# A two-layer transformer block on one NeuronCore: three norms between projections, run in two token halves

## The chip, the cores and the metric

The kernel runs on one core of one Trainium2 chip. The metric is the device time of one execution in microseconds (us). Of an execution the hardware profiler gives a span and, for each instruction, its engine, its start and its duration. The engines are TensorE (PE; its weight loads are PEld), VectorE (DVE), ScalarE (ACT), GpSimd (POOL) and SyncE (SP).

## The reference, cut to what matters

512 tokens of width 1024 go through two layers, all in float32. The three places of this change are where a projection with a residual is followed by an RMS norm and by the next stage's projections:

```python
# seam 1 (norm 1), first layer
x = x + jnp.concatenate([a, b], axis=-1) @ w_out[l]   # a: windowed attention, b: pooling mixer
h2 = rms_norm(x, norm2_g[l])
x = x + peer(h2, ...)                                 # begins with q = h2 @ wq
# rms_norm: y = x * rsqrt(mean(x * x, axis=-1) + eps) * g, each token over its 1024 values
```

Seams 2 and 3 (norms 4 and 6) are in the second part: the output projection of the differential attention (seam 2) and of the short convolution (seam 3), each scaled by a gate and added to x, then a norm with gain and shift, then a feed-forward that begins with its gate and up projections. Every token is normed for itself.

## The kernel before, in words

**Layout.** All activations lie with features on the 128 partitions and tokens along the free axis: x is 8 chunks (`DC = 8`) of 128 features by 512 tokens (`T`). The normed tokens are kept as a sum of two tiles, `hn_hi` and `hn_lo` (a rounded high part and the rest), and so is the input of the output projections, `mix_hi` and `mix_lo`.

**Weight units.** All weights come as 486 units of 128x1024 (`U_WIN` to `N_UNITS`), in the order of their use, through a ring of 8 slots (`RING`). SyncE loads unit u into slot u % 8 once `unit_used` says that unit u - 8 is used. ScalarE makes its high part (`split_hi`, L934), GpSimd its low part (L466), which overwrites the raw data, and TensorE waits for `lo_ready` (`unit_in`). ScalarE splits unit u + 5 (`AHEAD = 5`) when unit u has been used, so five units are ready ahead.

**A unit on TensorE.** `project` runs, for each of 8 chunks, three matmuls over 512 tokens (`mm3`, L494 to L496: high x high, high x low, low x high) into one PSUM bank, and then raises `unit_used`. Each unit gives 128 output features of all 512 tokens.

**The work around a seam.** Order is written out by hand for each engine; semaphores tie them together. The out projection is 8 units into 4 banks in turn. Behind each unit VectorE adds the bank to `x[:, n]` (L1425; with a gate L1689 in `add_projection`) and raises `x_done`; ScalarE splits a unit ahead and then squares chunk n - 1 of x (`square`, L948, called from `splits`); VectorE adds the square to `std` (`square_sum`, L1327). After the eighth unit:

- TensorE: `norm(k)` multiplies `std` by a matrix of ones, which sums over partitions (L515).
- ScalarE takes the square root (L960), VectorE its reciprocal (L1334), all for 512 tokens.
- Per chunk: VectorE scales x by gain and reciprocal into `nrm` (L1348), ScalarE writes the high part (L964, or L966 with a shift), VectorE the low part (L1339 or L1342) and raises `hn_ready`.
- TensorE's first unit of the next stage waits for each chunk in turn (`ready=`).

The next stage is the query projection of the expert layer at seam 1 (16 units, each followed by score matmuls, L602, and top-k work on VectorE, L1437 and below), and the feed-forward (`feed_forward`: `gate_up`, `down`) at seams 2 and 3. Norm 3, of 256 context tokens, runs through the same lines with tiles of 256 columns.

The lines of this order on VectorE and on ScalarE at seam 1 are:

```python
for n in range(DC):                                   # VectorE, L1423 to L1429
    dve.wait_ge(unit_used, U_WOUT + n + 1)
    V.tensor_tensor(x[:, n], ps[:, n % 4, :], x[:, n], ALU.add).then_inc(x_done, 1)
    if n > 1:
        square_sum(1, n - 1)
square_sum(1, DC - 1)
norm(1)

for m in range(n):                                    # ScalarE, splits(u0, n, k), L1029 to L1036
    used(u0 + m)
    split_hi(u0 + m + AHEAD)
    if m:
        square(k, m - 1)
square(k, DC - 1)
```

Of the kernel before, what the change touches and what calls it, by code (L numbers as in the profile page):

```python
# [16 lines left out]
F32 = mybir.dt.float32  # L17
# [3 lines left out]
ALU = mybir.AluOpType  # L21
# [88 lines left out]
def build_program(nc, w_units, x_in, ctx_in, params, consts, consts2, trig, pool_w, subkeys, ada_w, out,  # L110
                  rel_dram, gate_dram, act_dram, x_dram):
    KB = 1024
    with ExitStack() as ctx:
# [145 lines left out]
        SQUARES_BANK = (7, 7, 7, 7, 7, 0, 7)  # L259

# [20 lines left out]
        hn_ready = sem("hn_ready")  # L281
        hn_hi_ready = sem("hn_hi_ready")
# [106 lines left out]
        def _(sp):  # L389
# [43 lines left out]
            sp.wait_ge(hn_ready, 2 * DC)  # L433
# [51 lines left out]
        def _(pe):  # L485
# [25 lines left out]
            def norm(k):  # L511

                W = NORMS[k][1]
                pe.wait_ge(sq_added, (DC - 1) * (k + 1))
                mm(ps[:, SQUARES_BANK[k], :W], ones, std[:, :W], start=True, stop=True).then_inc(mean_ready, 1)  # L515

# [73 lines left out]
            for n in range(DC):  # L590
                if n >= 4:
                    pe.wait_ge(x_done, n - 3)
                project(U_WOUT + n, ps[:, n % 4, :], mix_hi, mix_lo)
            norm(1)


# [10 lines left out]
            for n in range(2 * PEER_HEADS):  # L607
                if n >= 4:
                    pe.wait_ge(q_ev, n - 3)
                project(U_WQ + n, ps[:, n % 4, :], hn_hi, hn_lo, ready=(hn_ready, DC) if n == 0 else None)  # L610
                if n:
                    scores(n - 1)
# [130 lines left out]
            def keys_own(n):  # L743
                unit_in(U_DIFF + n)
                for c in range(DC):
                    if n == 0:
                        pe.wait_ge(hn_ready, 2 * DC + c + 1)
# [3 lines left out]
            def keys_context(n):  # L751
                for c in range(DC):
                    if n == 0:
                        pe.wait_ge(hn_ready, 3 * DC + c + 1)
# [105 lines left out]
            def out_projection(u0, ready, ready0, x0):  # L860
                for n in range(DC):
                    if n >= 4:
                        pe.wait_ge(x_done, x0 + n - 3)
                    project(u0 + n, ps[:, n % 4, :], mix_hi, mix_lo, ready=(ready, ready0) if n == 0 else None)

            def feed_forward(L, U, x0):
                f0 = FF_TILES * L

                def gate_up(g, u, i=None, ready=None):
                    for k in range(2):  # L870
                        f = f0 + 2 * g + k
                        for a, s in ((0, ff_s), (1, ff_p)):
                            if f >= 2:
                                pe.wait_ge(s, f - 1 if i is None else i * 8 + (f - 1))
                            project(u + 2 * k + a, ps[:, 2 * a + k, :], hn_hi, hn_lo, per=24, i=i,
                                    ready=ready if k + a == 0 else None)
# [1045 lines left out]
```

## Time and profile before

| | |
|---|---|
| median of 3 runs | 3458.77 us |
| lowest and highest | 3450.98 and 3459.42 us |
| profiled execution, its own time | 3454.71 us |
| its span | 3452.9 us |
| mean granted clock of TensorE | 0.965 |

A row of the timeline gives the start in us from the span's start, the duration in us, the engine, the line, the operation, what is written from what is read, the shapes, and a count where several equal instructions were merged; square brackets hold the idle time before it and who ended it. A granted clock of 1.00 is 2.4 GHz and of 0.50 is 1.2 GHz. Matmuls are pipelined, so a record is longer than the distance to the next start. Durations on GpSimd are rough.

### The profile page before, as it was taken

To read this page: it belongs to the slowest core of one execution; us is meant where nothing else is said; L and a number is where in the kernel's file an instruction comes from. 1 tells how busy PE (TensorE), PEld (TensorE's weight loads), DVE (VectorE), ACT (ScalarE), POOL (GpSimd) and SP (SyncE) were. 2 spreads that over 40 slices of the span, in tenths; PEclk is the share of its full clock that TensorE was granted. 3 is DMA by queue.
4 is the path that set the end of the run, shared out by engine and by line. 5 is a ranking of instruction groups with operands and counts; after the bars stand their busy time and mean duration, and the time that the engine had idled before them with its cause. 6 is when DMAs were issued, how large, how long until landed. Compare 5 with 4: busy or idle time off the path is not lost.

```text
span 3452.9 us, 41466 instructions
## 1 busy us (share of the span) xinstructions
PE 3254.0 (94%) x14966; PEld 2584.8 (75%) x14966; DVE 1905.2 (55%) x2797; ACT 1099.3 (32%) x1524; POOL 1196.8 (35%) x490
## 2 busy tenths in 40 slices
PE   6689999999999989999999899898889998989999
PEld 4568668888888878888888678544568886868887
DVE  5548894666666525555555671778643336553333
ACT  3332233444444422222222332345322213222221
POOL 3123243333333344444444222100134443434442
PEclk9889999999999999999999999888899999999999
DMA  5022775555555565555555311100222222222222
GB/s 147 32 74 90 276 274 183 187 186 183 191 182 198 183 204 195 192 191 194 194 194 194 125 65 56 43 0 1 67 76 93 99 97 80 98 73 98 98 97 74
DMA packets 191913, 456.22 MB, mean 132 GB/s; under 512 B 11544, under 2 KB 79256, under 8 KB 189208
## 3 DMA queue, kind: packets, MB, share of 16 engines
q1 hardware_dynamic: 86688, 310.57, 26.3%
q10 hardware_dynamic: 105080, 143.66, 12.1%
q8 instruction: 97, 1.59, 0.2%
q14 instruction: 48, 0.39, 0.0%
HBM read 381.31 MB, written 72.88 MB: 132 GB/s over the span
## 4 chain that ended last, share of the span: by engine, by line
PE 83%; DVE 12%; ACT 2%; issue 1%; DMA 0%; ACTq 0%; SPq 0%; DVEq 0%
PE ps L494 25%; PE ps L495 25%; PE ps L496 25%; PE ps L658 3%; DVE nrm L1348 1%; PE ps L832 1%; PE ps L626 1%; DVE std L1327 1%; DVE stats L1601 1%; PE ps L814 1%; DVE Ed L1627 1%; DVE rstd L1334 1%; DVE dec L1484 1%; DVE hn_lo L1342 1%; PE ps L823 0%
## 5 line engine op out<-in xcount | busy, mean ns | idle before, releaser
L466 POOL TENSOR_TENSOR unit_lo<-unit_raw,unit_hi 128x1024 fp32r<-128x1024 f32 x486 | 1196.6, 2469 | 2229.6 <-ACT unit_hi L934 2228.5
L494 PE MATMUL ps<-hn_hi,unit_hi 128*128 128x512 f32 x2248 | 910.2, 405 | 52.4 <-DVE hn_lo L1342 31.7
L495 PE MATMUL ps<-hn_lo,unit_hi 128*128 128x512 f32 x2248 | 883.9, 393 | 0.0
L496 PE MATMUL ps<-hn_hi,unit_lo 128*128 128x512 f32 x2248 | 883.6, 393 | 0.0
L934 ACT ACTIVATE unit_hi<-unit_raw 128x1024 fp32r<-128x1024 f32 x486 | 504.6, 1055 | 661.2 <-DMA unit_raw<-w_units 498.1
L494 PEld LDWEIGHTS ps<-hn_hi,unit_hi 128*128 128x128 f32 x2248 | 426.9, 190 | 198.2 <-issue 69.9
L496 PEld LDWEIGHTS ps<-hn_hi,unit_lo 128*128 128x128 f32 x2248 | 426.8, 190 | 90.8
L495 PEld LDWEIGHTS ps<-hn_lo,unit_hi 128*128 128x128 f32 x2248 | 428.1, 190 | 85.4 <-issue 3.8
L494 PE MATMUL ps<-gp_hi,unit_hi 128*128 128x512 f32 x1024 | 399.3, 390 | 8.4 <-DVE gp_lo L1540 8.4
L495 PE MATMUL ps<-gp_lo,unit_hi 128*128 128x512 f32 x1024 | 399.2, 390 | 0.0
L496 PE MATMUL ps<-gp_hi,unit_lo 128*128 128x512 f32 x1024 | 399.1, 390 | 0.0
L1533 DVE TENSOR_TENSOR gp<-abuf,gbuf 128x512 f32<-128x512 f32 x128 | 232.6, 1818 | 238.6 <-PE ps L496 215.3
L1511 DVE TENSOR_SCALAR hotA<-con,eT 128x128 f32<-128x128 f32 x512 | 344.2, 732 | 0.0
L1704 DVE TENSOR_TENSOR pf<-gel,ps 128x512 f32<-128x512 f32 x44 | 30.3, 688 | 408.8 <-PE ps L496 408.8
L1069 ACT ACTIVATE stage<-ps 128x512 f32<-128x512 f32 x128 | 76.4, 597 | 561.3 <-PE ps L496 550.7
L1507 DVE TENSOR_TENSOR hotB<-con,eT 128x512 f32<-128x512 f32 x128 | 88.3, 690 | 265.6 <-PE ps L658 243.9
L494 PEld LDWEIGHTS ps<-gp_hi,unit_hi 128*128 128x128 f32 x1024 | 192.7, 188 | 48.8 <-issue 8.8
L496 PEld LDWEIGHTS ps<-gp_hi,unit_lo 128*128 128x128 f32 x1024 | 192.6, 188 | 40.1
L495 PEld LDWEIGHTS ps<-gp_lo,unit_hi 128*128 128x128 f32 x1024 | 192.7, 188 | 40.0
L1540 DVE TENSOR_TENSOR gp_lo<-gp,gp_hi 128x512 fp32r<-128x512 f32 x128 | 154.7, 1209 | 117.9 <-ACT gp_hi L1144 117.8
L1276 ACT ACTIVATE gel<-ps 128x512 f32<-128x512 f32 x44 | 26.3, 598 | 513.1 <-PE ps L496 513.1
L1718 DVE SCALAR_TENSOR_TENSOR x<-ps,modraw,x 128x512 f32<-128x512 f32 x176 | 126.4, 744 | 46.3 <-PE ps L496 45.1
(236 smaller groups left out, 3816.6 us busy)
## 6 DMA issues: line engine op xcount, KB each, us to landing
unit_raw<-w_units SPq DMA_DIRECT2D x486, 512.0 KB, 3.3
araw<-ada_units SPq DMA_DIRECT2D x96, 512.0 KB, 6.0
act_dram<-stage ACTq DMA_DIRECT2D x32, 1024.0 KB, 6.1
gate_dram<-gst ACTq DMA_DIRECT2D x16, 2048.0 KB, 8.1
gbuf<-gate_dram ACTq DMA_DIRECT2D x32, 1024.0 KB, 6.3
abuf<-act_dram ACTq DMA_DIRECT2D x32, 1024.0 KB, 9.9
x<-x_t SPq DMA_DIRECT2D x8, 256.0 KB, 6.0
x_dram<-x ACTq DMA_DIRECT2D x1, 2048.0 KB, 8.3
```

Source lines behind the costliest of these rows:

```text
L466: nc.gpsimd.tensor_tensor(lo[:, u % RING], raw[:, u % RING], hi[:, u % RING].bitcast(F32), ALU.subtract).then_inc(lo_ready, 1)
L494: mm(dst, wh, ah, start=start, stop=False)
L495: mm(dst, wh, al, start=False, stop=False)
L496: return mm(dst, wl, ah, start=False, stop=stop)
L658: last = mm(out_t, hotB[:, r % 2, j, :], hotA[:, r % 2, j, :], start=True, stop=True)
L934: activation(hi[:, u % RING], raw[:, u % RING], ACT.Copy).then_inc(hi_ready, 1)
L1069: activation(stage[:, g % 2, u % BUNCH], ps[:, u % 2, :], ACT.Gelu).then_inc(gel_done, 1)
L1507: V.tensor_tensor(hotB[:, r % 2], iota.unsqueeze(1).broadcast_to([P, 4, P]), four.unsqueeze(2).broadcast_to([P, 4, P]), ALU.is_equal)
L1511: last = V.tensor_scalar(hotA[:, r % 2, j, :], iota, eT[:, 0, tok], eT[:, 2, tok], ALU.is_equal, ALU.mult)
L1533: V.tensor_tensor(gp[:, v % 4].rearrange("p (b t) -> p b t", t=TB), abuf[:, g % 2, k].rearrange("p (b t) -> p b t", t=TB), gbuf[:, g % 2, ...
L1540: V.tensor_tensor(gp_lo[:, v % 4], gp[:, v % 4], gp_hi[:, v % 4].bitcast(F32), ALU.subtract).then_inc(p_ready, 1)
L1718: V.scalar_tensor_tensor(x[:, m], ps[:, 4 + m % 4, :], mod(L, 5)[:, m:m + 1], x[:, m], ALU.mult, ALU.add).then_inc(x_done, 1)
```

## The change

At the three seams the out projection, the norm and the first four units of the next stage are run for tokens 0 to 255 (half 0) and 256 to 511 (half 1):

- **TensorE** (`seam_projection`): the eight projection units for half 0, then the same eight for half 1, in three banks in turn; the squares of half 0 are multiplied by ones after the first half-1 unit. Then `seam_units`: the first four units of the next stage for half 0, waiting per chunk for half 0 of the normed tokens, with the squares of half 1 after the first of them; then the same four for half 1. `unit_used` is raised only in the half-1 passes.
- **ScalarE** (`seam`): three splits without a wait for a used unit during the first pass; in the second pass, behind unit n, the square of half 1's chunk n - 1, the high part of half 0's chunk n - 1, and from n = 3 on a split. At seam 1 the load of the sub-keys is issued before the projection instead of after it.
- **VectorE** (`seam`): in the second pass, behind unit n, the add of half 1, the sum of squares of half 1's chunk n - 1, the scaling of half 0's chunk n - 1 and the low part of half 0's chunk n - 2.
- The other four norms keep their code; their semaphore counts are renumbered (`WHOLE`). SyncE's first load of modulation weights waits for the half-counted semaphore. At seam 1 the scores of the first three units run in the half-1 pass (`after`).

The diff, cut to its core (`HALVES` are the two token slices, `SEAM` numbers the three seams):

```diff
+            def seam_projection(k, u0, x0, banks, ready=None):
+                for h in range(2):
+                    for n in range(DC):
+                        j = DC * h + n
+                        if j >= DC + 3:
+                            pe.wait_ge(x_done, x0 + n - 2)
+                        elif j >= 3:
+                            pe.wait_ge(half_added, DC * SEAM[k] + j - 2)
+                        unit_in(u0 + n)
+                        for c in range(DC):
+                            if ready is not None and j == 0:
+                                pe.wait_ge(ready, c + 1)
+                            wh, wl = unit_chunk(u0 + n, c)
+                            last = mm3(ps[:, banks[j % 3], 0:T // 2], wh, wl, mix_hi[:, c, HALVES[h]],
+                                       mix_lo[:, c, HALVES[h]], c == 0, c == DC - 1)
+                        last.then_inc(unit_used if h else half_full, 1)
+                        if j == DC:
+                            seam_mean(k, 0)
+            def seam_units(k, u0, banks, after=None):
+                for h in range(2):
+                    for n, bank in enumerate(banks):
+                        unit_in(u0 + n)
+                        for c in range(DC):
+                            if n == 0:
+                                pe.wait_ge(half_ready, DC * (2 * SEAM[k] + h) + c + 1)
...
+                        if h:
+                            last.then_inc(unit_used, 1)
+                            if n and after is not None:
+                                after(n - 1)
+                        elif n == 0:
+                            seam_mean(k, 1)
...
-                project(U_WOUT + n, ps[:, n % 4, :], mix_hi, mix_lo)
-            norm(1)
+            seam_projection(1, U_WOUT, 0, (4, 5, 6))
...
+            seam_units(1, U_WQ, range(4), after=scores)
...
-            out_projection(U_WO, wo_lo, 0, X_WO)
-            norm(4)
+            seam_projection(4, U_WO, X_WO, (4, 5, 6), ready=wo_lo)
...
+            def seam(k, u0):
+                for n in range(DC):
+                    if n < DC - AHEAD:
+                        split_hi(u0 + n + AHEAD)
+                    if n:
+                        seam_square(k, 0, n - 1)
+                seam_square(k, 0, DC - 1)
+                activation(rstd[:, 0:1], eps, ACT.Sqrt)
+                for n in range(DC):
+                    used(u0 + n)
+                    if n == 0:
+                        seam_root(k, 0)
+                    else:
+                        seam_square(k, 1, n - 1)
+                        seam_high(k, 0, n - 1)
+                    if n >= DC - AHEAD:
+                        split_hi(u0 + n + AHEAD)
+                seam_square(k, 1, DC - 1)
+                seam_high(k, 0, DC - 1)
+                seam_root(k, 1)
+                for c in range(DC):
+                    seam_high(k, 1, c)
...
+            def seam(k, u0, banks, gate=None):
...
+                for n in range(DC):
+                    add(0, n)
+                    if n > 1:
+                        sum_up(0, n - 1)
+                sum_up(0, DC - 1)
+                for n in range(DC):
+                    add(1, n)
+                    if n == 0:
+                        inverse(0)
+                        continue
+                    if n > 1:
+                        sum_up(1, n - 1)
+                    scaled(0, n - 1)
+                    if n > 1:
+                        low(0, n - 2)
+                sum_up(1, DC - 1)
+                scaled(0, DC - 1)
+                low(0, DC - 2)
+                low(0, DC - 1)
+                inverse(1)
+                for c in range(DC):
+                    scaled(1, c)
+                    if c:
+                        low(1, c - 1)
+                low(1, DC - 1)
```

## Rows read from the trace of the kernel before

**Rows 1.** The page's first part: busy time of each engine.

```profile
PE 3254.0 (94%) x14966; PEld 2584.8 (75%) x14966; DVE 1905.2 (55%) x2797; ACT 1099.3 (32%) x1524; POOL 1196.8 (35%) x490
```

**Rows 2.** Timeline of TensorE at seam 1: start, duration, line, operation, [idle before].

```profile
179.04 0.50 PE L494 MATMUL ps<-mix_hi,unit_hi 128*128 128x512 f32 x1 [1.41 <-DVE mix_lo L1420]
...
227.78 2.08 PE L515 MATMUL ps<-std,con 128*128 128x512 f32 x2 [4.91 <-DVE std L1327]
236.28 0.77 PE L494 MATMUL ps<-hn_hi,unit_hi 128*128 128x512 f32 x1 [6.43 <-DVE hn_lo L1339]
...
246.11 0.39 PE L494 MATMUL ps<-hn_hi,unit_hi 128*128 128x512 f32 x1
```

**Rows 3.** Timeline of TensorE, two matmuls of 512 columns, 168 apart.

```profile
183.94 0.39 PE L494 MATMUL ps<-mix_hi,unit_hi 128*128 128x512 f32 x1
...
222.02 0.39 PE L494 MATMUL ps<-mix_hi,unit_hi 128*128 128x512 f32 x1
```

**Rows 4.** Stretches at seam 1: length, busy times, granted clock, DMA share, GB/s.

```profile
224.00:226.00 2.00, 0.00 (x0) 0.00 (x0) 1.49 (x1) 1.98 (x3) 1.97 (x1) 0.72 0.90 307
...
240.00:241.00 1.00, 1.00 (x4) 0.56 (x3) 0.96 (x2) 0.36 (x1) 0.00 (x0) 0.50 0.00 0
...
242.00:244.00 2.00, 1.65 (x6) 0.80 (x6) 1.96 (x4) 0.73 (x2) 0.00 (x0) 1.00 0.00 0
```

**Rows 5.** Timeline of TensorE, two matmuls of 256 columns, 47 starts apart.

```profile
2087.69 0.28 PE L494 MATMUL ps<-unit_hi,cn_hi 128*128 128x256 f32 x1
...
2093.33 0.28 PE L496 MATMUL ps<-unit_hi,cn_lo 128*128 128x256 f32 x1
```

**Rows 6.** Timeline behind a unit of seam 1; last row: GpSimd idle.

```profile
195.70 1.06 ACT L934 ACTIVATE unit_hi<-unit_raw 128x1024 fp32r<-128x1024 f32 x1 [3.86 <-PE ps L496]
...
196.66 0.61 ACT L948 ACTIVATE sq<-x 128x512 f32<-128x512 f32 x1
196.84 2.40 POOL L466 TENSOR_TENSOR unit_lo<-unit_raw,unit_hi 128x1024 fp32r<-128x1024 f32 x1 [3.05 <-ACT unit_hi L934]
197.31 2.47 DVE L1327 TENSOR_TENSOR std<-std,sq 128x512 f32<-128x512 f32 x1 [0.92 <-ACT sq L948]
...
1958.91 0.68 DVE L1327 TENSOR_TENSOR std<-std,sq 128x512 f32<-128x512 f32 x1
```

**Rows 7.** Timeline of GpSimd and VectorE in norm 0, two GpSimd operations merged.

```profile
27.38 5.47 POOL L466 TENSOR_TENSOR unit_lo<-unit_raw,unit_hi 128x1024 fp32r<-128x1024 f32 x2 [4.01 <-ACT unit_hi L934]
...
30.68 2.73 DVE L1348 SCALAR_TENSOR_TENSOR nrm<-x,par,rstd 128x512 f32<-128x512 f32 x1
```

**Rows 8.** Timeline of GpSimd and VectorE in the first feed-forward, merged rows.

```profile
2561.95 10.11 POOL L466 TENSOR_TENSOR unit_lo<-unit_raw,unit_hi 128x1024 fp32r<-128x1024 f32 x4 [6.12 <-ACT unit_hi L934]
...
2569.71 3.52 DVE L1718 SCALAR_TENSOR_TENSOR x<-ps,modraw,x 128x512 f32<-128x512 f32 x5
```

**Rows 9.** Timeline of norm 3, whose tiles have 256 columns.

```profile
1987.83 0.47 ACT L960 ACTIVATE std<-ps,con 128x256 f32<-128x256 f32 x1 [1.83 <-PE ps L515]
...
1988.33 1.75 DVE L1334 RECIPROCAL rstd<-std 128x256 f32<-128x256 f32 x1 [1.82 <-ACT std L960]
1990.12 0.88 DVE L1348 SCALAR_TENSOR_TENSOR nrm<-cT,gmod,rstd 128x256 f32<-128x256 f32 x2
...
1990.64 0.91 ACT L966 ACTIVATE cn_hi<-nrm,gmod 128x256 fp32r<-128x256 f32 x2 [2.34 <-DVE nrm L1348]
```

**Rows 10.** Seam 2: the last low parts; second unit of the feed-forward.

```profile
2462.97 1.47 DVE L1670 TENSOR_TENSOR mix_lo<-Od,mix_hi 128x512 fp32r<-128x512 f32 x2
...
2527.39 0.40 PE L494 MATMUL ps<-hn_hi,unit_hi 128*128 128x512 f32 x1
```

**Rows 11.** Seam 3: the last low part beside GpSimd; second unit of the feed-forward.

```profile
3029.72 2.39 POOL L466 TENSOR_TENSOR unit_lo<-unit_raw,unit_hi 128x1024 fp32r<-128x1024 f32 x1 [3.05 <-ACT unit_hi L934]
...
3029.84 2.83 DVE L1759 TENSOR_TENSOR mix_lo<-yc,mix_hi 128x512 fp32r<-128x512 f32 x1
...
3095.95 0.39 PE L494 MATMUL ps<-hn_hi,unit_hi 128*128 128x512 f32 x1
```

**Rows 12.** Timeline of VectorE in the query projection: the top-k behind a unit.

```profile
259.00 0.89 DVE L1437 MAX8 vals<-ps 128x8 f32<-128x128 f32 x4 [1.11 <-PE ps L602]
```

More of the change, by code:

```diff
@@ L513, in norm, with seam_mean @@
                 W = NORMS[k][1]
-                pe.wait_ge(sq_added, (DC - 1) * (k + 1))
+                pe.wait_ge(sq_added, (DC - 1) * (WHOLE[k] + 1))
                 mm(ps[:, SQUARES_BANK[k], :W], ones, std[:, :W], start=True, stop=True).then_inc(mean_ready, 1)
+            def seam_mean(k, h):
+                pe.wait_ge(half_summed, (DC - 1) * (2 * SEAM[k] + h + 1))
+                mm(ps[:, SQUARES_BANK[k], HALVES[h]], ones, std[:, HALVES[h]], start=True, stop=True)\
+                    .then_inc(half_mean, 1)
@@ L606, in _ @@
             pe.wait_ge(subk_in, 16)
[L607 to L612, printed above, removed]
+            seam_units(1, U_WQ, range(4), after=scores)
+            for n in range(4, 2 * PEER_HEADS):
+                pe.wait_ge(q_ev, n - 3)
+                project(U_WQ + n, ps[:, n % 4, :], hn_hi, hn_lo)
+                scores(n - 1)
             scores(2 * PEER_HEADS - 1)
@@ L858, in _, with gate_up @@
             at_squares(HEADS - 1)
[L860 to L864, printed above, removed]
             def feed_forward(L, U, x0):
                 f0 = FF_TILES * L
-                def gate_up(g, u, i=None, ready=None):
+                def gate_up(g, u, i=None):
                     for k in range(2):
@@ L872, in gate_up @@
                         for a, s in ((0, ff_s), (1, ff_p)):
[L873 to L876, printed above, removed]
+                            pe.wait_ge(s, f - 1 if i is None else i * 8 + (f - 1))
+                            project(u + 2 * k + a, ps[:, 2 * a + k, :], hn_hi, hn_lo, per=24, i=i)
                 def down(g, u, i=None):
@@ L1027, in _ @@
                            ACT.Copy).then_inc(swa_hi, 1)
-            def splits(u0, n, k):
-                for m in range(n):
-                    used(u0 + m)
-                    split_hi(u0 + m + AHEAD)
-                    if m:
-                        square(k, m - 1)
-                square(k, DC - 1)
-            splits(U_WOUT, DC, 1)
+            act.wait_ge(swa_lo, TT)
             act.dma_start(subk[:, :, :], subkeys).then_inc(subk_in, 16)
-            norm(1)
+            seam(1, U_WOUT)
             o, w = PAR["c"]
@@ L1291, in feed_forward @@
                     split_hi(U + 64 + k + AHEAD)
-            splits(U_WO, DC, 4)
-            norm(4)
+            seam(4, U_WO)
             feed_forward(0, U_FF0)
@@ L1304, in _ @@
                     split_hi(U_SC + 3 * j + a + AHEAD)
-            splits(U_SCO, DC, 6)
-            norm(6)
+            seam(6, U_SCO)
             feed_forward(1, U_FF1)
@@ L1421, in _ @@
                                 mix_hi[:, 0:4, tok].bitcast(F32), ALU.subtract).then_inc(swa_lo, 1)
-            for n in range(DC):
-                dve.wait_ge(unit_used, U_WOUT + n + 1)
-                V.tensor_tensor(x[:, n], ps[:, n % 4, :], x[:, n], ALU.add).then_inc(x_done, 1)
-                if n > 1:
-                    square_sum(1, n - 1)
-            square_sum(1, DC - 1)
-            norm(1)
+            seam(1, U_WOUT, (4, 5, 6))
             V.memset(cact[:, :, :], 0.0).then_inc(cact_made, 1)
@@ L1736, in _ @@
                 dve.wait_ge(loaded, 16)
-            add_projection(U_WO, mod(0, 2), 4)
-            norm(4)
+            seam(4, U_WO, (4, 5, 6), mod(0, 2))
             feed_forward(0, U_FF0, X_FF0)
@@ L1759, in _ @@
                 V.tensor_tensor(mix_lo[:, j], yc[:, b], mix_hi[:, j].bitcast(F32), ALU.subtract).then_inc(sc_done, 1)
-            add_projection(U_SCO, mod(1, 2), 6)
-            norm(6)
+            seam(6, U_SCO, (6, 4, 5), mod(1, 2))
             feed_forward(1, U_FF1, X_FF1)
```

114 lines of the change are left out of this document (85 added, 29 removed).

## The prediction

> **What bounds the kernel now.** TensorE: the page's first part has it busy for 94% of the span [rows 1]. I looked next at what it does around one of the three norms, in the timeline. At the first seam the eight units of the out projection start at 179.04, the matmul over the squares comes at 227.78 after 4.91 us of idleness, the first matmul on the normed tokens at 236.28 after 6.43 more, and the second unit of the next stage at 246.11 [rows 2]. A unit is 24 matmuls of 512 columns; the gap from 183.94 to 222.02 is 168 of them, so 0.2267 us each and 5.44 a unit [rows 3]. Nine units should take 49.0 us, and 246.11 - 179.04 is 67.1: 18 us are lost at this seam, in idleness and in a first unit fed chunk by chunk. The stretches show the granted clock: it falls to 0.50 (1.2 GHz) in the gap, stays there with TensorE waiting, and is 1.00 (2.4 GHz) again from about 242, some 5.5 us after work resumed [rows 4]. The two other seams look alike. So there is something to win, at most 3 x 18 us; the question is what the halves cost and whether the vector work fits beside them.
>
> **What the halves cost on TensorE.** A matmul of 256 columns starts every (2093.33 - 2087.69) / 47 = 0.120 us [rows 5], so a half unit is 2.88 us and a whole one in halves 5.76, 0.32 more. Twelve units a seam run in halves: 3.8 us a seam, 11.5 in all. The Trainium skill (TensorE: Matmul & The Clock Gate, "Back-to-back issue gap") gives N/2.4 + 2.5 ns, about 109 and 216 ns; by that the halving would cost an estimated 2 us in all. The rows disagree with it, and the rows decide.
>
> **The lock between VectorE and GpSimd.** Every weight unit needs a high part (ScalarE, L934) and then a low part (GpSimd, L466, 2.40 us). In the timeline of the first seam the split starts at 195.70, GpSimd at 196.84, the square ends at 197.27, and the add of squares std+sq, started at 197.31, takes 2.47 us where it takes 0.68 with GpSimd idle: it ends 0.54 us after GpSimd's end at 199.24 [rows 6]. All six such adds beside a low part in each seam look so. The loser waits for the whole instruction. The same holds for a scaling (L1348: 2.73 instead of 0.75), and after two queued GpSimd operations it shows VectorE getting its turn between them [rows 7]. Adds out of PSUM pass untouched: five of L1718 in 3.52 us while GpSimd runs from 2561.95 to 2572.06 [rows 8]. Before, one such wait per 5.44 us unit was hidden.
>
> In the second half pass of the new order this is on the chain. From the fourth unit on ScalarE does, in this order: square(n-1) of half 1, high part of chunk n-1 of half 0, split of weights; VectorE does add, sum, scaling, low part. The split releases GpSimd (2.40), the square after it releases the sum, which meets the lock each time; the scaling stands behind the sum on VectorE, the high part behind the scaling, and the next split behind the high part on ScalarE. One round, from GpSimd's start to its next: 2.40, then 0.27 until the scaling starts (half of the 0.54 above, the width being half), 0.48 + 0.04 for it, 0.41 from the start of the high part to the split behind it (two of 256 columns in 0.91 us), and 1.14 from the split to GpSimd's start (196.84 - 195.70): 4.74 us [rows 6, 9]. TensorE needs only 2.88. There are five splits, so four rounds.
>
> **The chain of a later seam**, counted from T0, the end of the first half pass. Eight half units and the matmul over squares (about 0.5, a quarter of the 2.08 us of [rows 2]: half the columns, twice the clock): second pass ends at 23.5. The fourth of its units ends at 12.0; add, sum, scaling and high part (0.48 + 0.42 + 0.48 + 0.40, with 0.2 of handing over) bring the first split to 14.0 and GpSimd to 15.1. Four rounds later it starts at 34.0 and ends at 36.4. Behind it are sum, scaling and two low parts (0.27 + 3 x 0.48 + 0.1): chunk 7 of half 0 is ready at 38.3, nearly 15 us after TensorE could use it. TensorE then ends its first unit at 38.8, does the second matmul over squares and three more half units (8.64): 47.9. Meanwhile half 1: square root 0.47, reciprocal 1.75, then two operations of 0.48 per chunk, as in the norm of 256 columns [rows 9]: ready by about 50.0, the last chunk of the next unit being wanted at 50.4, so hidden. Four more half units end at 59.4. The first seam has shorter forms (no shift; Copy), 58.7.
>
> **The clock.** During the wait TensorE does 0.36 us of work per round, so I take its clock to fall as it does now and to be at 1.2 GHz for about 5 us after 38.3. Before, this lay under the feeding by chunks; now TensorE has work queued. 256 columns at 1.2 GHz take an estimated 0.213 us against the 0.120 of [rows 5], so each us at that clock does 0.44 us less work: 2.2 a seam. Bounds: 0 if the clock stays up, and open above (second rival).
>
> **The start of a seam.** At the later two the first unit waits for the last chunks of its own input; today 6 or 7 chunks of 0.68 us hide in that wait, then only 0.36 each. At the second seam the last low part ends at 2464.44 [rows 10], so the first half unit ends at 2465.0 and T0 is 2485.2 (seven times 2.88). At the third the last low part, itself blocked by GpSimd, ends at 3032.67 [rows 11]; half unit at 3033.2, T0 3053.4. The splits now issue there without waiting for a used unit, so GpSimd has its next operation queued behind that low part; by [rows 7] VectorE goes first, and at worst it costs 2.4 us once. The sub-key DMA moved ahead on ScalarE's queue is one issue while ScalarE waits for TensorE anyway, and lands earlier than it is wanted; the reload of x before seam 2 delays the first add to where three banks still cover it; SyncE's own waits see later slots (eight units are held for a whole pass), but each is split some 11 us after it is freed, and a transfer lands within a few: hidden. Three PSUM banks instead of four: TensorE waits for an add three half units back, at most 5 us behind: hidden.
>
> **The sum**, to the end of the fourth unit of the next stage (second unit's start now + 3 x 5.44 = 16.3):
> - Seam 1: now 246.11 + 16.3 - 179.04 = 83.4; then 0.1 (the first matmul takes 0.50, not 0.39) + 23.0 + 58.7 + 2.2 = 84.0: +0.6.
> - Seam 2: now 2527.39 [rows 10] + 16.3 = 2543.7; then 2485.2 + 59.4 + 2.2 = 2546.8: +3.1.
> - Seam 3: now 3095.95 [rows 11] + 16.3 = 3112.3; then 3053.4 + 59.4 + 2.2 = 3115.0: +2.7.
>
> Together +6.4. It reaches the end whole: after seam 1 VectorE's top-k idles 1.11 us per unit behind TensorE [rows 12], and the feed-forwards run at TensorE's pace. Against the profiled execution's 3454.7 us this gives 3461; the runs lie between 3451.0 and 3459.4, their median 4 us above it, so I say 3462. About 0.3% (10 us) is what a measurement of this kernel can tell from no change.
>
> **Rivals.**
> - The lock doesn't set the pace (0.14). If the short operations slip past GpSimd, a round is under 2.88 us, chunk 7 is ready near 28.7 and the clock stays up: 59.4 becomes 49.9, 58.7 becomes 49.7. Seams -10.6, -8.6, -9.0, together -28: 3427. For it: 256-column operations are short. Against: all 18 adds beside GpSimd in [rows 6]'s pattern.
> - The clock comes back late (0.22), slower. It costs 0.44 us per us at 1.2 GHz, in all three seams; beyond 8 us cold a seam the total is over +10. With 12 it is +16: 3471. For it: TensorE's gaps before the restart are longer than now. Against: it took 5.5 us in [rows 4].
> - Half units cost just half of whole ones (0.03). Then 0.16 us is off each of the 19 half units a seam that count (8 in the first pass, 4 until the first split, 7 behind the wait), 9 us in all: 3453. [rows 5] speak against it. By the spacing of the Trainium skill cited above it would be nearly so.
> - The forecast, a chain of vector work taking the place of the idle gap: 0.61.
>
> **Numbers.** Round length off by 0.3 us is +-3.6 over twelve rounds; the clock 0 to +10; the runs' own spread 4 each side. 3447 to 3474 leaves out the first rival and little above. Faster is the first rival, 0.14; slower the second and a sliver of the forecast's upper part, 0.25; the rest, 0.61, within 0.3%.
>
> **What would show it.** Right: sums of 256 columns at about 2 us or more beside GpSimd in the second pass, GpSimd starts 4.7 us apart, TensorE waiting some 13 us on hn_lo in its first unit at each seam, half-clock matmuls after it, 0.12 us between warm ones. The forecast is wrong if GpSimd starts come 2.9 us apart and the wait on hn_lo is under 6 us a seam, or if half the clock lasts over 8 us.

## The result, and the profile after

The changed kernel takes 3460.8 us (median of 20 runs, 3456.2 to 3462.1) against 3455.6 (3451.0 to 3459.4) for the kernel before: a ratio of 1.0013, 95% interval 1.0007 to 1.0019. It is 5 us slower, which lies within the 0.3% called no change; 3462 was forecast. The profiled execution has a span of 3458.8 us against 3452.9.

So three idle gaps of TensorE were filled, and nothing was won. The page's first part shows the halves' cost: 870 matmul instructions more, and 12 us more of busy time than in [rows 1].

```profile
PE 3266.3 (94%) x15836; PEld 2641.6 (76%) x15836; DVE 1931.2 (56%) x2893; ACT 1112.2 (32%) x1575; POOL 1194.0 (35%) x490
```

The timeline of TensorE after, at seam 1, answers to [rows 2]. The columns are start, duration, line, operation, and in brackets the idle time before it and what ended it.

```profile
182.65 0.39 PE L501 MATMUL ps<-mix_hi,unit_hi 128*128 128x256 f32 x1 [1.41 <-DVE mix_lo L1567]
208.66 0.59 PE L527 MATMUL ps<-std,con 128*128 128x256 f32 x2
...
229.24 0.28 PE L501 MATMUL ps<-hn_hi,unit_hi 128*128 128x256 f32 x1
...
233.21 0.39 PE L501 MATMUL ps<-hn_hi,unit_hi 128*128 128x256 f32 x1 [2.38 <-DVE hn_lo L1469]
237.70 0.58 PE L501 MATMUL ps<-hn_hi,unit_hi 128*128 128x256 f32 x1 [3.87 <-DVE hn_lo L1469]
242.20 0.58 PE L501 MATMUL ps<-hn_hi,unit_hi 128*128 128x256 f32 x1 [3.48 <-DVE hn_lo L1469]
243.65 1.05 PE L527 MATMUL ps<-std,con 128*128 128x256 f32 x2
```

The first mean (208.66) no longer costs a wait: the wait of 4.91 us on the squares and the one of 6.43 us on the first normed chunk are gone. The next stage begins at 229.24 with four chunks at once (12 matmuls), and then TensorE waits three times on low halves, ahead of chunks 4, 5 and 6: 9.7 us in all (10.2 at each later seam). The first norm's last chunks come only at 242.20, 13 us after the stage began.

One round of that wait, in the timeline of all engines (weight loads and matmuls left out), shows why:

```profile
229.78 2.37 POOL L473 TENSOR_TENSOR unit_lo<-unit_raw,unit_hi 128x1024 fp32r<-128x1024 f32 x1 [2.15 <-ACT unit_hi L970]
...
230.05 2.38 DVE L1451 TENSOR_TENSOR std<-std,sq 128x256 f32<-128x256 f32 x1 [1.07 <-ACT sq L1015]
...
232.35 0.47 DVE L1462 SCALAR_TENSOR_TENSOR nrm<-x,par,rstd 128x256 f32<-128x256 f32 x1
...
232.86 0.42 ACT L1029 ACTIVATE hn_hi<-nrm 128x256 fp32r<-128x256 f32 x1 [2.85 <-DVE nrm L1462]
233.08 0.41 DVE L1441 TENSOR_TENSOR x<-ps,x 128x256 f32<-128x256 f32 x1
233.18 1.04 ACT L970 ACTIVATE unit_hi<-unit_raw 128x1024 fp32r<-128x1024 f32 x1
...
234.30 2.34 POOL L473 TENSOR_TENSOR unit_lo<-unit_raw,unit_hi 128x1024 fp32r<-128x1024 f32 x1 [2.15 <-ACT unit_hi L970]
```

GpSimd starts its low part at 229.78; VectorE's sum of 256 columns begins 0.27 us later and takes 2.38 us. Behind it stand the scaling (232.35), behind that the high half (232.86) and the next split of weights (233.18), and GpSimd starts again at 234.30: a round of 4.52 us where TensorE's half unit takes 2.88.

The stretches after (columns: length, busy time and count of TensorE, its weight loads, VectorE, ScalarE and GpSimd, granted clock, DMA share, GB/s) answer to [rows 4]:

```profile
239.00:242.00 3.00, 0.00 (x0) 0.00 (x0) 2.95 (x3) 0.18 (x2) 2.13 (x1) 0.50 0.00 0
242.00:244.00 2.00, 1.80 (x7) 1.78 (x8) 0.57 (x2) 0.26 (x1) 0.00 (x0) 0.50 0.00 0
244.00:246.00 2.00, 2.00 (x10) 1.84 (x9) 0.75 (x1) 0.47 (x1) 0.00 (x0) 0.52 0.00 0
246.00:247.00 1.00, 1.00 (x10) 1.00 (x10) 1.00 (x1) 0.00 (x0) 0.00 (x0) 1.00 0.02 8
```

The granted clock fell to 0.50 (1.2 GHz) in the waits and stayed there for 3.8 us after the restart, with matmuls queued.

Per seam, from its first matmul to the start of the fifth unit of the next stage: seam 1 took 85.2 us (267.87 - 182.65) against 86.0 (265.06 - 179.04), seam 2 92.0 (2547.77 - 2455.78) against 88.5, seam 3 85.5 (3118.12 - 3032.63) against 83.9. That is -0.8, +3.5 and +1.6, together +4.3 of the 5.1 us between the medians. What lies between the seams differs by some us from one profiled execution to the next (between seams 1 and 2 it is 2190.2 us in the kernel before and 2187.9 in the changed one; run 10 below shows one wait behind it), so below the seams are compared inside each trace and the medians beside them.

### The profile page after: what moved, and what is told of

Its sections match the earlier page's. It is cut to its first block, busy times and chain, and to the rows that moved or that the text cites. A ratio compares the mean times of both kernels' runs of the same rounds, so it can differ in the third digit from the quotient of the medians.

```text
span 3458.8 us, 43404 instructions
## 1 busy us (share of the span) xinstructions
PE 3266.3 (94%) x15836; PEld 2641.6 (76%) x15836; DVE 1931.2 (56%) x2893; ACT 1112.2 (32%) x1575; POOL 1194.0 (35%) x490
## 4 chain that ended last, share of the span: by engine, by line
PE 86%; DVE 9%; ACT 2%; issue 1%; DMA 1%; ACTq 0%; SPq 0%; DVEq 0%
PE ps L501 26%; PE ps L502 25%; PE ps L503 25%; PE ps L704 3%; PE ps L672 1%; DVE std L1451 1%; DVE stats L1742 1%; PE ps L878 1%; DVE Ed L1768 1%; PE ps L860 1%; DVE nrm L1424 1%; PE ps L681 1%; DVE std L1403 1%; DVE nb L1723 0%; ACT unit_hi L970 0%
## 5 line engine op out<-in xcount | busy, mean ns | idle before, releaser
L501 PE MATMUL ps<-hn_hi,unit_hi 128*128 128x512 f32 (+1 forms) x2344 | 926.9, 395 | 58.9 <-DVE hn_lo L1471 20.5
L502 PE MATMUL ps<-hn_lo,unit_hi 128*128 128x512 f32 (+1 forms) x2344 | 901.6, 385 | 0.0
L503 PE MATMUL ps<-hn_hi,unit_lo 128*128 128x512 f32 (+1 forms) x2344 | 900.9, 384 | 0.0
L501 PEld LDWEIGHTS ps<-hn_hi,unit_hi 128*128 128x128 f32 x2344 | 447.4, 191 | 190.9 <-issue 46.2
L503 PEld LDWEIGHTS ps<-hn_hi,unit_lo 128*128 128x128 f32 x2344 | 447.4, 191 | 86.8
L502 PEld LDWEIGHTS ps<-hn_lo,unit_hi 128*128 128x128 f32 x2344 | 448.1, 191 | 82.9 <-issue 3.8
L1681 DVE TENSOR_TENSOR gp_lo<-gp,gp_hi 128x512 fp32r<-128x512 f32 x128 | 165.9, 1296 | 119.9 <-ACT gp_hi L1222 119.7
```

The lines of the kernel that those rows point to most:

```text
L501: mm(dst, wh, ah, start=start, stop=False)
L502: mm(dst, wh, al, start=False, stop=False)
L503: return mm(dst, wl, ah, start=False, stop=stop)
L1681: V.tensor_tensor(gp_lo[:, v % 4], gp[:, v % 4], gp_hi[:, v % 4].bitcast(F32), ALU.subtract).then_inc(p_ready, 1)
```

## The experiments

Twelve kernels ran; each time is the median of 4 to 11 executions. Changes are given against the changed kernel's 3460.8 us unless said otherwise; "tail" is the sum over the three seams of the time from the first mean to the fifth unit of the next stage, 174.8 us in the changed kernel (59.2 + 57.9 + 57.7).

**1. GpSimd only writes in the second pass.** The kernel leaves the low parts of 15 of the 486 weight units out of the products.

```diff
+                if i is None and any(b <= u < e for b, e in ((U_WOUT + 8, U_WOUT + 13), (U_WO + 8, U_WO + 13),
+                                                             (U_SCO + 8, U_SCO + 13))):
+                    nc.gpsimd.memset(lo[:, u % RING].bitcast(F32), 0.0).then_inc(lo_ready, 1)
+                    return
                 nc.gpsimd.tensor_tensor(lo[:, u % RING], raw[:, u % RING], hi[:, u % RING].bitcast(F32),
```

> The changed kernel in which GpSimd, for the five units whose low parts it makes in the second pass of each seam (15 units of 768 in all), only writes zeros into the low tile: it reads nothing. That leaves the low part of these 15 weight units out of the products. Theory (VectorE's two-input operations and GpSimd's subtract exclude each other, which sets a round of about 4.55 us in the second pass): the chunk sums fall from 2.36-2.47 us to about 0.42, the waits of TensorE on the low halves (2.4 to 4.0 us, three in a seam) go, the rounds fall to the half unit's 2.88 us, and the kernel comes out about 28 us under the changed one (25 to 35), near 3432. Rival (the lock is no limit; ScalarE or the start of the stage sets the pace): within 5 us of the changed kernel. If the fill takes the same port, the sums stay long but for the fill's own length, and the gain lies in between.

Measured 3430.6 us, -30.2 (ratio to the kernel before 0.9923, 0.9910 to 0.9937). The tail is 147.4 us, -27.4. VectorE's groups of instructions between 218 and 250 us (busy time, mean ns of one, idle before), and GpSimd's timeline:

```profile
L1460 DVE TENSOR_TENSOR std<-std,sq 128x256 f32<-128x256 f32 x6 | 2.6, 425 | 1.5 <-ACT sq L1024 1.4
```

```profile
225.85 0.96 POOL L474 MEMSET unit_lo<- 128x1024 f32 x1 [1.92 <-ACT unit_hi L979]
228.73 0.96 POOL L474 MEMSET unit_lo<- 128x1024 f32 x1 [1.92 <-ACT unit_hi L979]
```

The same group in the changed kernel:

```profile
L1451 DVE TENSOR_TENSOR std<-std,sq 128x256 f32<-128x256 f32 x6 | 12.1, 2010 | 4.7 <-ACT sq L1015 4.6
```

The sum falls from a mean of 2010 to 425 ns, and GpSimd's starts stand 2.88 us apart, TensorE's own pace. Of the three waits one is left, of 1.9 us. The Trainium skill (SBUF — State Buffer, "Who interferes with whom") says that a VectorE instruction with two SBUF inputs contends with a GpSimd instruction that reads SBUF and not with one that only writes it; the run agrees, the sums standing at 0.42 us beside fills of 0.96. The fill is also shorter than the subtract, 0.96 us for 2.40, so this run changes two things. But 2.40 us would fit into TensorE's 2.88, so GpSimd's length by itself doesn't make a round of 4.5; the sum that stands behind it does, and runs 4 to 7, which keep every subtract, bear that out.

**2. The control: the same fill in the kernel before**, for units +5 to +12 of each seam, whose low parts it leaves out of the products.

```diff
+                if i is None and any(b <= u < e for b, e in ((U_WOUT + 5, U_WOUT + 13), (U_WO + 5, U_WO + 13),
+                                                             (U_SCO + 5, U_SCO + 13))):
+                    nc.gpsimd.memset(lo[:, u % RING].bitcast(F32), 0.0).then_inc(lo_ready, 1)
+                    return
```

> The control: the kernel before with the same fill in place of GpSimd's subtract, in the eight units of each seam whose low parts are made while the norm's chain runs (24 units; their low parts are left out of the products). Theory: in the kernel before the lock holds up only the last sums and the first scaled products of each seam, one blocked sum each of about 1.8 us, so the time falls by 3 to 8 us at most against the kernel before. Rival (GpSimd's subtract costs the same in either kernel, for instance through TensorE's late weights): as large a fall as in the changed kernel, about 28 us.

Measured 3447.1 us, 8.8 under the kernel before (0.9974, 0.9965 to 0.9983), a little over the upper end named. The wait on the squares falls from the 4.91 us of [rows 2]; the waits of TensorE around seam 1 (in total, times, longest) now have:

```profile
PE ps L524 <- DVE std L1336: 3.2, 1, 3.2
```

That is 1.7 us a seam, 5.2 of the 8.8 in all; the rest was not taken apart. The lock cost the order before under 9 us and the new one 30: the change brought some 21 us of it onto the path.

**3. The halves alone, in the order before.**

```diff
+                for h in (slice(0, T // 2), slice(T // 2, T)):
                     for c in range(DC):
-                        last = mm3(dst, wh, wl, ah[:, c], al[:, c], c == 0, c == DC - 1)
+                        last = mm3(dst[:, h], wh, wl, ah[:, c, h], al[:, c, h], c == 0, c == DC - 1)
```

> The kernel before, in its own order, but 31 of the units that the change cuts are computed as two token halves back to back by TensorE alone (8+3, 7+3, 7+3; each weight is loaded twice). It prices the cut itself. By the rows (0.12 us for a matmul of 256 columns against 0.2267 for one of 512, 24 pairs in a unit: 0.32 us a unit) the kernel is about 10 us slower than before (8 to 12). Rival (two halves cost what the whole does): within 2 us of the kernel before.

Measured 3465.3 us, 9.5 over the kernel before (1.0028, 1.0018 to 1.0039), for 31 units: 0.31 us a unit. Its timeline has the matmuls of 256 columns 45 starts apart in 5.40 us, 0.120 each:

```profile
189.83 0.28 PE L494 MATMUL ps<-mix_hi,unit_hi 128*128 128x256 f32 x1
...
195.23 0.28 PE L494 MATMUL ps<-mix_hi,unit_hi 128*128 128x256 f32 x1
```

**4. Two of five splits later.** ScalarE splits the fourth unit of the next stage behind the first norm's last high half, and the fifth behind the second norm's.

```diff
-                    if n >= DC - AHEAD:
+                    if DC - AHEAD <= n < DC - 2:
                         split_hi(u0 + n + AHEAD)
                 seam_square(k, 1, DC - 1)
                 seam_high(k, 0, DC - 1)
+                split_hi(u0 + DC - 2 + AHEAD)
                 seam_root(k, 1)
                 for c in range(DC):
                     seam_high(k, 1, c)
+                split_hi(u0 + DC - 1 + AHEAD)
```

> The changed kernel with two of the five high-part splits of each second pass issued later on ScalarE: that of the fourth unit of the next stage after the last high half of the first norm, that of the fifth after the second norm's high halves. GpSimd then makes three low parts in the second pass and two behind it. Theory (the lock sets the pace, each low part in the pass holds up VectorE by some 2 us): two fewer collisions in each pass, less the one that moves behind, so 6 us less a seam, 9 if TensorE's clock stays up, 18 to 27 us under the changed kernel. Rival (what paces the pass is something else): within 5 us of the changed kernel, or slower where the fourth unit's weight now comes late (up to 5 us a seam).

Measured 3439.9 us, -20.9; the tail is 157.2, -17.6. The weights did not come late.

**5. The sum last on VectorE.**

```diff
-                    if n > 1:
-                        sum_up(1, n - 1)
                     scaled(0, n - 1)
                     if n > 1:
                         low(0, n - 2)
-                sum_up(1, DC - 1)
+                        sum_up(1, n - 1)
                 scaled(0, DC - 1)
                 low(0, DC - 2)
                 low(0, DC - 1)
+                sum_up(1, DC - 1)
```

> The changed kernel with VectorE's order in the second pass turned round: in each round the scaled product and the low half of the first norm come ahead of the sum of the second norm's squares, and at the end the two last low halves come ahead of the last sum. The same operations, the same collisions with GpSimd. Theory: in the changed kernel the sum is the operation that sits out the lock (2.36 us a round) and it stands ahead of the low half for which TensorE waits; with the sum behind, the first norm's halves come up to one blocked operation earlier at the end (about 4.4 us a seam), so some 13 us under the changed kernel (8 to 16). Rival (the order in a round does not matter, since the round is as long as before): within 3 us of the changed kernel.

Measured 3441.3 us, -19.5, more than the 8 to 16 expected; the tail is 158.6, -16.2. VectorE at seam 2:

```profile
2505.03 0.47 DVE L1462 SCALAR_TENSOR_TENSOR nrm<-x,gmod,rstd 128x256 f32<-128x256 f32 x1
2505.43 0.47 DVE L1471 SCALAR_TENSOR_TENSOR hn_lo<-nrm,modraw,hn_hi 128x256 fp32r<-128x256 f32 x1
2505.82 2.58 DVE L1451 TENSOR_TENSOR std<-std,sq 128x256 f32<-128x256 f32 x1
2508.32 2.55 DVE L1462 SCALAR_TENSOR_TENSOR nrm<-x,gmod,rstd 128x256 f32<-128x256 f32 x1
```

Scaling and low half slip by ahead of the sum, which takes the wait. With two low parts queued on GpSimd the lock catches the next scaling too (2.55 us). So it does in every other round (scalings of 1.84 us at 2495.13 and 2.23 at 2501.76); in the rounds between, the chain of scaling, high half and split holds no blocked operation. GpSimd's starts stand 4.26, 2.57, 4.43 and 2.53 us apart: its fourth low part at seam 2 starts 11.3 us after the first (2494.29 to 2505.55), where the changed kernel has 13.9 (2501.93 to 2515.82). That second effect was missing from the expectation.

**6. Both together.** Both diffs, that of run 4 and this one:

```diff
                     if n > 1:
                         low(0, n - 2)
+                        sum_up(1, n - 1)
```

> Both of the last: two of the five splits of each second pass later on ScalarE, and VectorE's sum last in each round. Theory: both remove blocked operations from ahead of the first norm's halves, about 11 us a seam together, so 33 us under the changed kernel (27 to 37), near 3428, which is under the kernel before too. Rival (the two save the same wait): no more than the late splits alone, 3440.

Measured 3429.3 us, -31.5; the tail is 145.7, -29.1. Of 20.9 + 19.5 = 40.4 us, 31.5 came: the two are for the most part different waits, and some of them the same.

**7. Three splits later, and the sum last.** The third split of the pass moves behind the first norm's last high half too.

```diff
-                    if DC - AHEAD <= n < DC - 2:
+                    if DC - AHEAD <= n < DC - 3:
                         split_hi(u0 + n + AHEAD)
                 seam_square(k, 1, DC - 1)
                 seam_high(k, 0, DC - 1)
+                split_hi(u0 + DC - 3 + AHEAD)
                 split_hi(u0 + DC - 2 + AHEAD)
```

> As the last, with three of the five splits later: only the first two stay in the second pass, the third and fourth come after the first norm's last high half, the fifth after the second norm's. Theory: one collision fewer in the pass, about 1 us a seam under the last, so near 3425 (3418 to 3430). Rival (the fourth unit's low part now comes later than TensorE needs it, and GpSimd's queue becomes the bound): slower than the last by up to 2 us a seam.

Measured 3423.8 us, -37.0 (0.9911, 0.9897 to 0.9924 to the kernel before). The tail is 139.1 us, -35.8. Nearly nothing of the waits is left at seam 2. The second mean is back at 0.59 us, and the granted clock is 1.00 in every stretch from 2480 to 2515:

```profile
2500.42 0.39 PE L501 MATMUL ps<-hn_hi,unit_hi 128*128 128x256 f32 x1 [0.34 <-DVE hn_lo L1474]
2501.55 0.59 PE L527 MATMUL ps<-std,con 128*128 128x256 f32 x2
2513.20 0.38 PE L501 MATMUL ps<-hn_hi,unit_hi 128*128 128x256 f32 x1 [0.27 <-DVE hn_lo L1474]
```

Seven half units, eight more and two means are 43.7 us of TensorE's own work (15 x 2.88 + 2 x 0.24); this tail has 45.8. In the tails it beats run 1 (147.4), in which GpSimd doesn't lock at all but the order is the change's; between the totals, 3423.8 and 3430.6, the intervals overlap.

**8. TensorE kept busy in its waits, first attempt.**

```diff
+                            if h == n == 0 and c > 4:
+                                for _ in range((16, 28, 24)[c - 5]):
+                                    mm(ps[:, banks[1], HALVES[0]], wh, hn_hi[:, c - 1, HALVES[0]], start=True, stop=True)
```

> The changed kernel in which TensorE, ahead of its three waits in the first unit of the next stage (chunks 5, 6 and 7), multiplies 16, 28 and 24 further matmuls of 256 columns into a bank that is not read before it is written anew (some 1.9, 3.4 and 2.9 us of waits of 2.4 to 4.0 us). Nothing is left out. Theory for the clock: the granted clock stays at its upper level through the waits, the mean takes 0.59 us and not 1.05, the matmuls after the restart stand 0.12 us apart at once, and the kernel is about 6.6 us under the changed one (2.2 us a seam; 4 to 8). Rival (the clock falls for another reason than the idle time, or its fall costs nothing since the waits are long anyway): within 2 us, or slower if the extra matmuls outlast the waits.

Measured 3482.4 us, +21.6: a miss, and not a test of the clock. The waits stand ahead of chunks 4, 5 and 6, so the matmuls ahead of chunk 7 met no wait and were pure delay. That is a few us. The larger part lies outside the seams. TensorE's waits from 300 to 1400 us (in total, times, longest):

```profile
PE ps L503 <- issue: 12.4, 3, 4.6
PE ps L698 <- DVE sel L1634: 3.2, 1, 3.2
```

"Issue" is time in which no engine's work is awaited. The three waits are of 4.57, 4.58 and 3.21 us (at 709.49, 882.93 and 1055.14), each 5 to 6 us behind one of three short "issue" waits (0.4 to 0.9 us) that come 167 to 174 us apart in this stage with and without the addition. Behind each the granted clock is lower too: 0.91, 0.83 and 0.83 in the 20 us around them, against 1.00. The changed kernel has neither row. From the fifth unit at seam 1 to the first matmul of seam 2 this kernel takes 2209.6 us, the changed one 2187.9.

**9 and 10. The same, put right**, in seams 2 and 3 alone (run 9; run 10 has no `and k > 1`).

```diff
+                            if h == n == 0 and c in (4, 5, 6) and k > 1:
+                                for _ in range((10, 17, 15)[c - 4]):
+                                    mm(ps[:, banks[1], :], wh, mix_hi[:, c, :], start=True, stop=True)
```

> The run on TensorE's clock again, with what the first one had wrong put right: the waits stand ahead of chunks 4, 5 and 6 (not 5, 6 and 7), so the further matmuls go there: 10, 17 and 15 of 512 columns (2.3, 3.9 and 3.4 us of waits of 2.4 to 2.7, 3.9 and 3.5 us), and only in seams 2 and 3, so that the program ahead of the expert loop is the changed kernel's. Nothing is left out. Theory: the clock stays at its upper level, the second mean takes 0.59 us and not 1.05, and each of the two seams is 2.2 us shorter than in the changed kernel, 4.4 in all (3456.4; 3 to 6). Rival (the fall costs nothing, or the busy TensorE disturbs something else): within 2 us of the changed kernel or slower.

> The same further matmuls in all three seams. Theory A: seam 1 gains its 2 us too, 3454. Theory B, from the first such run, whose expert loop between 600 and 1000 us held three waits of TensorE of 4 us each that no engine's work ended: a longer program ahead of the loop moves the loop to addresses where its instructions come late, and the stage between 300 and 1400 us is longer than in the changed kernel by 10 to 20 us, so that the total comes out at 3465 to 3475 although seam 1 is shorter.

Run 9: 3456.2 us, -4.6 (0.9999, 0.9990 to 1.0008, which just touches the changed kernel's 1.0007 to 1.0019). Seam 2 in it; L558 is the added matmuls:

```profile
2512.98 0.39 PE L501 MATMUL ps<-hn_hi,unit_hi 128*128 128x256 f32 x1 [0.45 <-DVE hn_lo L1474]
2513.45 4.01 PE L558 MATMUL ps<-mix_hi,unit_hi 128*128 128x512 f32 x17
2517.61 0.39 PE L501 MATMUL ps<-hn_hi,unit_hi 128*128 128x256 f32 x1 [0.15 <-DVE hn_lo L1474]
2518.08 3.56 PE L558 MATMUL ps<-mix_hi,unit_hi 128*128 128x512 f32 x15
2522.26 0.39 PE L501 MATMUL ps<-hn_hi,unit_hi 128*128 128x256 f32 x1 [0.61 <-DVE hn_lo L1474]
2523.38 0.60 PE L527 MATMUL ps<-std,con 128*128 128x256 f32 x2
```

The stretch of the last of these waits, with the granted clock in the third column from the end:

```profile
2520.00:2524.00 4.00, 3.34 (x18) 2.47 (x17) 2.68 (x4) 0.51 (x1) 1.12 (x1) 1.00 0.00 0
```

The chunks arrive as late as before; only the clock is different (1.00 through the whole wait), and the tails of the two seams are 2.0 and 1.8 us shorter. The second mean takes 0.60 us and not 1.05. Run 10: 3457.7 us, -3.1. Seam 1's tail is 1.3 us shorter too, yet the total is no better than run 9's and not Theory A's 3454; the intervals overlap. Theory B falls for this size of addition: the waits for "issue" did not return with 42 instructions more at seam 1. What made them in run 8 stays open. The wait of 3.2 us on VectorE's selection (L698) did return, in run 10's waits; the second row is from the kernel before:

```profile
PE ps L698 <- DVE sel L1634: 3.2, 1, 3.2
PE ps L649 <- DVE sel L1490: 3.4, 1, 3.4
```

So it isn't tied to the added matmuls: of the fourteen profiled executions those of the kernel before and of runs 8, 10 and 12 have it, at about 511 us (502 in run 12), and the other ten don't. The stretch between seams 1 and 2 is 2190 to 2193 us in the three of them other than run 8 and 2185 to 2189 in the rest. What brings it is not shown; it blurs the comparison of totals by some 3 us.

**11 and 12. The start of a seam.** Run 7, and TensorE multiplies the first chunks of the second half unit before it waits for the last chunks of its input: seven chunks ahead of chunk 7 in both later seams (run 11), six ahead of chunk 6 in seam 2 (run 12, whose `ahead` is 6 at seam 2 and 7 at seam 3). The diff is run 12's.

```diff
+                                if c == ahead:
+                                    unit_in(u0 + 1)
+                                    for e in range(ahead):
+                                        wh, wl = unit_chunk(u0 + 1, e)
+                                        mm3(ps[:, banks[1], 0:T // 2], wh, wl, mix_hi[:, e, HALVES[h]],
+                                            mix_lo[:, e, HALVES[h]], e == 0, False)
                                 pe.wait_ge(ready, c + 1)
```

> The best version so far (later splits, sum last), and at the start of seams 2 and 3 TensorE multiplies chunks 0 to 6 of the first two half units before it waits for the last chunk of its input. Theory (the start of a seam costs more by halves, since a half unit of 2.88 us covers less of the wait for the last chunk than a whole one of 5.44): the waits of 4.3 us (seam 2) and 1.65 us (seam 3) take in 2.5 us of work, so seam 2 gains 2.5 us, and up to 1.5 more where the clock stays up, and seam 3 1.6: 3 to 6 us under the last version, near 3419. Rival (the second unit's weights or the adds behind it are the limit there): within 1.5 us of it.

> The same as the last, put right for seam 2: the trace shows that TensorE waits there ahead of chunk 6 (18 matmuls of the first half unit, then 4.30 us), so the second half unit's chunks 0 to 5 go ahead of chunk 6 in seam 2 (seam 3 stays as it was, ahead of chunk 7). Theory: these 18 matmuls take 3.8 us at the lower clock, all of it within the 4.3 us, and are then missing behind it: from the end of that wait to the first mean 2.2 to 3.8 us less than the last run's 25.5 us, and 3417 in all (3415 to 3419). Rival (the adds or the weights of the third unit are then the limit): within 1 us of the last run, 3420.

Run 11: 3420.1 us, 3.7 under run 7. At seam 3 the wait of 1.65 us is gone. At seam 2 nothing changed, because the wait stands ahead of chunk 6:

```profile
2440.61 0.55 PE L501 MATMUL ps<-mix_hi,unit_hi 128*128 128x256 f32 x1 [1.48 <-DVE mix_lo L1821]
2449.09 0.58 PE L501 MATMUL ps<-mix_hi,unit_hi 128*128 128x256 f32 x1 [4.30 <-DVE mix_lo L1821]
...
2474.58 0.59 PE L527 MATMUL ps<-std,con 128*128 128x256 f32 x2
```

Run 12, the same stretch:

```profile
2447.26 0.55 PE L501 MATMUL ps<-mix_hi,unit_hi 128*128 128x256 f32 x1 [1.47 <-DVE mix_lo L1822]
2455.74 0.39 PE L501 MATMUL ps<-mix_hi,unit_hi 128*128 128x256 f32 x1 [1.58 <-DVE mix_lo L1822]
...
2477.86 0.59 PE L527 MATMUL ps<-std,con 128*128 128x256 f32 x2
```

The chunk arrives 8.48 us after the start in both; the first mean follows 22.1 us later (2477.86 - 2455.74) and not 25.5: 3.4 us, within the 2.2 to 3.8 expected. The whole kernel takes 3418.9 us (0.9892, 0.9875 to 0.9908), 1.2 under run 11, with intervals that overlap: the gain is shown in the trace of the seam and not resolved in the total. The execution that was profiled is the longest of run 12's four (3421.75) and has the wait on VectorE's selection; run 11's has not. It is the fastest of the kernels run, 36.7 us under the kernel before and 41.9 under the changed one.

## Why the prediction was right

The case forecast is the one that came, for the reason given, and most terms hold.

**The halves.** 0.120 us a matmul and 0.32 us a unit were read from [rows 5]; run 3 gives 0.31. The spacing that the Trainium skill gives for an isolated matmul (TensorE: Matmul & The Clock Gate, "Back-to-back issue gap") would have made the halving an estimated 2 us in all; run 3 measures 9.5 for 31 of 36 units, so the third rival is out. For a stream of 512 columns the same section of the Trainium skill has about 131 ns a matmul, which the prediction didn't weigh; [rows 3] show 226.7.

**The lock.** Forecast was a round of 4.74 us; measured are 4.49 to 4.56 at seam 1 and 4.58 to 4.65 at seam 2. The sum's share was as forecast; the link that was shorter is from the high half to the split, 0.32 us (232.86 to 233.18) where 0.41 was taken, the rest being hundredths in each link. The last chunk was to be ready 38.3 us after T0; TensorE resumed 36.4 us after it at seam 1 (242.20 - 205.8) and 36.9 at the others. Part of that is the end of the chain, where 1.8 us were taken from GpSimd's last end to TensorE's restart and 1.1 came. The waits on hn_lo add up to 9.7 and 10.2 us, where the text wanted some 13. That the lock sets the pace, and not merely accompanies it, is shown by run 1, in which the rounds are 2.88 us, together with runs 4 to 7. The first rival gave 3427 for a pass without the lock; run 1 gives 3431. Its mechanism was sized rightly, its condition was not met.

**The clock.** 2.2 us a seam were taken from a spacing estimated at 0.213 us and 5 us at the lower level. The lower level lasted 3.8 to 5.5 us after the restart, and runs 9 and 10 put the cost at 1.3, 2.0 and 1.8 us. The second rival (over 8 us cold) did not come.

**The start of a seam.** The third seam's first mean came where it was forecast, to 0.1 us once the later start is taken off. At the second it came 1.2 us late: the text counted the clock only in the second pass. TensorE enters this seam at the lower level in both kernels. Two stretches of the kernel before, then two of the changed one:

```profile
2459.00:2461.00 2.00, 2.00 (x6) 1.54 (x6) 1.97 (x2) 0.00 (x0) 0.00 (x0) 0.60 0.00 0
2461.00:2463.00 2.00, 1.10 (x5) 0.56 (x3) 1.93 (x4) 0.00 (x0) 0.00 (x0) 1.00 0.00 0
```

```profile
2456.00:2460.00 4.00, 3.96 (x18) 3.67 (x18) 4.00 (x6) 0.32 (x1) 0.00 (x0) 0.50 0.22 92
2460.00:2464.00 4.00, 0.00 (x0) 0.00 (x0) 3.90 (x5) 0.36 (x1) 0.00 (x0) 0.50 0.00 0
```

The whole unit had the clock back at 1.00 ahead of its wait of 1.60 us. The half unit runs out of chunks first: it waits 4.30 us at 0.50, and its matmuls stand 0.21 us apart, the lower level's spacing, until 2467.99, 3.7 us after the wait's end at 2464.26. Run 12 fills 2.7 us of this wait, and its clock is at 1.00 in the stretch from 2454 on.

**The sum.** Forecast +0.6, +3.1 and +2.7; measured -0.8, +3.5 and +1.6. At seam 1 both sides of the sum lack a term: the three sets of score matmuls that run before the fifth unit, 2.6 us. The kernel before takes 86.0 us there and not 83.4, the changed one 85.2 and not 84.0; the term falls out of the difference. From T0 (the first mean's start less a half unit) to the fifth unit the later seams took 60.8 and 60.6 us where 61.6 was forecast. The total is +6.4 against +4.3 in the seams and +5.1 in the medians. In a sum of terms of 23 to 60 us a seam an error of 1 to 2 us is small partly by luck: the two sides cancel nearly. Luck too is in the 3462, for the base was chosen between an execution of 3454.7 us and a median of 3458.8; twenty runs put the kernel before at 3455.6.

What the prediction did not ask is whether the new order must have the lock in it. It named the lock as the bound and priced it at some 35 us (-28 for a pass without it, +6.4 with it; run 1 gives 30), but it took the place of the five splits and of the sum as given. Runs 4 to 7 move them and get it all back.

## What to carry to other kernels

A gap filled by cutting work in halves is won only if the vector work that must fit in the halves does, and its pace is set by its slowest link; here an engine pair that excludes each other put a 2.4 us operation ahead of a 0.4 us one in every round. Before such a change is dropped, look which operation waits for the lock and what is queued behind it: putting the operation nobody waits for last, and moving the other engine's work past the critical pass, turned +5 us into -32. A shorter first piece of work also covers less of the wait for its last input, so the start of a stage needs a second piece to go on with.

## What was not expected of the hardware

- 42 matmuls a seam whose product nobody reads make the stage shorter: 2.0 and 1.8 us in the tails of run 9 (-4.6 us in its total). Without them the granted clock comes back to 1.00 only 3.8 to 5.5 us after the last wait.
- A kernel with 204 short matmuls more had three waits of 3.2 to 4.6 us in another stage, for nothing that the trace names (run 8), and the one with 126 wider ones had none. The added work cost far more than its own time there; whether by the program's length or by something else was not found.
